# A new order of the second block's branches, and ten of its projection tiles in three FP32R passes

## The chip, the cores and the metric

The kernel runs on one core of a Trainium2 chip. The metric is the device time of one execution in microseconds, all inputs in HBM at the start and the output there at the end.

## What is computed

Two blocks follow each other on x, 256 tokens of 1024 channels, all in float32. The first is a hybrid layer (two attentions, a recurrence, spatial gating, four gated branch products and `merged @ w_out`). The second mixes with three branches and ends in a mixture of experts. Cut to what matters here:

```
hx = modulate(rmsnorm(x, norm1_g), mod[0], mod[1])
z  = hx @ w_in                       # hyena 768, HGRN 5*512 (q, f_fwd, f_bwd, i, g), Fourier 256 columns

# hyena: short convolution over tokens, then twice a product with a long bidirectional convolution
v, x1, x2 = split(short_conv3(z_hy)); h = hyena_filters(...)
y = x1 * fftconv(v, h[:, 0], h[:, 1]); y = x2 * fftconv(y, h[:, 2], h[:, 3]); y_hy = rmsnorm(y)

# HGRN: gated linear attention in both directions, 4 heads of 128
scores = einsum("bhtd,bhsd,bhtsd->bhts", q, k, decay);  o = scores @ v + carried state
y_hg = rmsnorm_per_head(o) * silu(g)

# Fourier: FFT over tokens and channels, real part, a small product
y_fn = rmsnorm(einsum(fftn(z_fn).real, fn_w) + fn_b)

x = x + mod[2] * (concat(y_hy, y_hg, y_fn) @ w_out)
h = modulate(rmsnorm(x), ...)
experts = router(h)                  # 2 of 16, within the best of 4 groups
x = x + mod[5] * sum over experts of combine * ((silu(h @ w_gate) * (h @ w_up)) @ w_down)
out = rmsnorm(x)
```

## The kernel before

One list, `PLAN`, names all jobs of the kernel: `("hg_set", 3)` is level 3 of HGRN's preparation. Each engine has its own functions for a job's name (`@part(TENSOR, "hg_set")` and so on), and each engine's program is made by walking through `PLAN` in order and emitting its part. Nothing reorders later: an engine does its jobs strictly in the order of `PLAN` and waits, at semaphores, for the jobs of others. `woven(main, fill)` puts one job of `fill` behind each job of `main`. The eight PSUM banks are handed out in turn in TensorE's order of jobs.

Activations lie with channels on the partitions. A weight matrix arrives in pieces of 2 MB (1024 x 512), each in one of three slots in SBUF; SyncE issues the loads in the order of first use in `PLAN`, and waits before each until the last user of the slot is done. One tile of a projection, `("channels", name, i)` (`tensor_channels`, L637), is 128 output channels x 256 tokens: eight fp32 matmuls of 128 x 256, each shown as two in the records. `("tokens", "v2", tt)` (L618) is the same for 128 tokens x 512. The names are f0, f1 (the forget gates), q2, v2, g2 (HGRN), hy0 (4 tiles), hy1 (2) and fn (2).

A product in three FP32R passes (`three_passes`, L1334 to L1336) splits both factors in a high and a low part, high x high, low x high and high x low: 24 matmuls per tile instead of 8, each faster than fp32. The high part of a weight tile is a copy by ScalarE (`scalar_split`, L1318), the low part is weight minus high by VectorE (`vector_split`, L1324), into a home in SBUF for the high part and over the weights in their slot for the low part. Before the change, out1, the first block's gated products and out2 are computed so.

The second block's mixer:

- `norm h2` makes the normed input; f0, f1 and q2 (12 tiles) are woven with the hyena filter: `filter_in` (L1538, a sine on ScalarE and VectorE between the two layers, L1562), `taps` (L1569) and `response` (L1596).
- `hg_start` (L1630, L1632 on VectorE) and `hg_diagonal` (scores of the diagonal). Then levels 0 to 7: `hg_set L` prepares the factors of a level on VectorE (six operations of 128x512: L1686, L1687, L1690, L1692, L1686, L1687) and GpSimd (two, L1698 and L1700, which prepare the second direction's state for the next level); `hg_scores L` is eight matmuls on TensorE (L1638) and two masked copies on VectorE (L1717). `sets` has two buffers, so set L waits for scores L-2.
- `hy_conv j` (VectorE, L1813 and twice L1816) is the short convolution of tile j, `hy_tokens n` turns it (L1827), `hy_freq o ft` is half of the forward transform (L1846; products L1860, L1861, L1863, L1864 on VectorE), `hy_time o` the inverse (L1877 or L1879; the gate L1889 or L1892).
- `fourier_in`, `fourier_turn`, `fourier_out` (L1902, L1919, L1934); `hg_out`, `hg_norm` (L1748, L1750, L1768), `hg_close` (Newton steps L506, L508, L510 on 128x1024, L1793, L1798).
- `norm2` (L1962) for hyena and Fourier; `cat_split` (ScalarE L1988, VectorE L1994) makes high and low parts of the branches' results for out2. `router_fold` (L2050), `out2` 0 to 7, `x_turn` (L2063, L2064).

In `PLAN` before, v2, g2, hy0, hy1, the convolutions and fn are the fill between the levels, and hyena's transforms, hg_out, hg_norm, norm2 and hg_close stand behind all of it.

Behind x_turn the router picks experts; the expert weights are loaded in an order that depends on its result, so SyncE waits for VectorE's L2648 before the first of them.

## Time and profile before

| | |
|---|---|
| median of 3 runs | 1199.16 us (1197.82 to 1199.33) |
| profiled execution, its time and its span | 1197.87 us, 1196.0 us |
| granted TensorE clock, mean of the span | 0.927 |
| TensorE busy | 1038.1 us (87%) |
| VectorE, ScalarE, GpSimd busy | 567.4 us (47%), 395.7 us (33%), 46.5 us (4%) |
| the chain that ended last | TensorE 72%, VectorE 13%, DMA 8%, ScalarE 4% |
| first projection tile of the second block | 610.75 us |
| last turn of x ends | 852.0 us |
| first load of an expert's weights issued | 869.92 us |
| hg_start on VectorE (L1630, L1632) | 0.70 + 1.23 us |
| router_fold on TensorE (L2050) | 1.85 us |
| a load of `w_in`, issue to landing, median | 8.3 us |

A span is the time from the first to the last recorded instruction of the profiled execution; durations and starts are all from that one execution. TensorE has two levels of clock, 1.2 and 2.4 GHz; the granted clock is the mean share of the higher one. Consecutive instructions overlap a little in the records, so the time of one in a row of many is the distance between starts, and the busy time of a row is slightly longer.

### The profile page before, as it was taken

The page shows a single profiled execution, that of the slowest core. Times are in us where ns is not written, and L with a number is a line of the kernel's source. Part 1 is how long each engine was busy: PE and PEld are TensorE (multiplying, and loading weights), DVE is VectorE, ACT ScalarE, POOL GpSimd, SP SyncE. Part 2 cuts the span into 40 slices and gives each one's busy share as a digit, 9 for nine tenths or more (in the row PEclk, how much of TensorE's full clock was granted, in tenths as well). Part 3 has the DMA queues.
Part 4 walks back from the last instruction along what each step waited for, and adds up shares of the span by engine and source line. Part 5 has one row for each costly group of instructions (what it writes and reads, how often), then busy time and mean ns, then how long its engine had stood idle before and what let it go on. Part 6 is the DMA issues. An engine that isn't in the chain of part 4 may idle for free.

```text
span 1196.0 us, 13332 instructions
## 1 busy us (share of the span) xinstructions
PE 1038.1 (87%) x5422; PEld 758.2 (63%) x5422; DVE 567.4 (47%) x1031; ACT 395.7 (33%) x664; POOL 46.5 (4%) x66
## 2 busy tenths in 40 slices
PE   5989897797879799989989995837788999999984
PEld 3465785564459689859967694736776565366531
DVE  2363324754345464515542167285584341277815
ACT  2222342643136454314351100212463230256501
POOL 1000000000000000000000022000000000000001
PEclk9999897899789899999989997978789999999988
DMA  9623163046971474356224213000187999799994
GB/s 303 185 93 107 47 224 129 1 141 229 387 298 71 141 253 158 140 198 208 71 94 141 95 48 140 1 1 1 58 333 301 325 349 387 291 404 409 408 388 158
DMA packets 110347, 230.63 MB, mean 193 GB/s; under 512 B 8236, under 2 KB 15693, under 8 KB 110286
## 3 DMA queue, kind: packets, MB, share of 16 engines
q1 hardware_dynamic: 104080, 216.44, 49.9%
q0 software_dynamic: 2880, 9.71, 2.1%
q10 hardware_dynamic: 3326, 3.63, 1.0%
q8 instruction: 43, 0.70, 0.2%
q14 instruction: 18, 0.15, 0.0%
HBM read 221.11 MB, written 8.65 MB: 192 GB/s over the span
## 4 chain that ended last, share of the span: by engine, by line
PE 72%; DVE 13%; DMA 8%; ACT 4%; issue 2%; POOL 0%; ACTq 0%; DVEq 0%; SPq 0%; POOLq 0%
PE bank L637 16%; PE bank L618 8%; PE bank L2398 5%; PE bank L1334 4%; PE bank L1335 4%; PE bank L1336 4%; PE bank L2337 4%; PE bank L2338 4%; PE bank L2339 4%; PE bank L2422 3%; DMA slot<-in_ada_w 3%; DMA more_slots<-in_moe_w_up 2%; DMA slot<-in_w_in 2%; PE bank L2330 2%; PE bank L1377 2%
## 5 line engine op out<-in xcount | busy, mean ns | idle before, releaser
L637 PE MATMUL bank<-x_and_h,slot 128*128 128x256 f32 x768 | 178.5, 390 | 4.9 <-ACT x_and_h L546 4.9
L637 PEld LDWEIGHTS bank<-x_and_h,slot 128*128 128x128 f32 x768 | 147.7, 195 | 32.2 <-issue 9.9
L1335 PE MATMUL bank<-rounded 128*128 128x256 f32 x480 | 136.2, 284 | 0.0
L1334 PE MATMUL bank<-rounded 128*128 128x256 f32 x416 | 121.5, 292 | 4.0 <-DVE slot_rounded L1324 4.0
L618 PE MATMUL bank<-slot,x_and_h 128*128 128x512 f32 x224 | 99.3, 601 | 4.5 <-DVE x_and_h L583 4.5
L1335 PEld LDWEIGHTS bank<-rounded 128*128 128x128 f32 x480 | 91.8, 191 | 0.3
L1336 PE MATMUL bank<-rounded,slot_rounded 128*128 128x256 f32 x296 | 84.3, 285 | 0.0
L1334 PEld LDWEIGHTS bank<-rounded 128*128 128x128 f32 x416 | 79.7, 192 | 6.3 <-issue 5.5
L1324 DVE TENSOR_TENSOR slot_rounded<-slot,rounded 128x1024 fp32r<-128x1024 f32 (+1 forms) x53 | 55.1, 1061 | 58.2 <-ACT rounded L1318 57.9
L618 PEld LDWEIGHTS bank<-slot,x_and_h 128*128 128x128 f32 x224 | 42.8, 193 | 56.1 <-issue 55.1
L647 ACT ACTIVATE arena<-bank 128x256 f32<-128x256 f32 x56 | 21.5, 385 | 145.3 <-PE bank L637 145.2
L1318 ACT ACTIVATE rounded<-slot 128x1024 fp32r<-128x1024 f32 (+1 forms) x53 | 47.5, 923 | 32.1 <-PE bank L1336 22.1
L2726 DVE TENSOR_TENSOR hidden<-hidden,bank 64x512 f32<-64x512 f32 (+3 forms) x19 | 12.9, 686 | 93.4 <-ACT hidden L2532 62.1
L1336 PEld LDWEIGHTS bank<-rounded,slot_rounded 128*128 128x128 f32 x296 | 57.1, 193 | 0.0
L2688 DVE TENSOR_TENSOR slot_rounded<-slot,weights_high 128x1024 fp32r<-128x1024 f32 x38 | 45.3, 1220 | 17.4 <-ACT weights_high L2499 17.0
L2499 ACT ACTIVATE weights_high<-slot 128x1024 fp32r<-128x1024 f32 x38 | 39.2, 1056 | 21.7 <-PE bank L2339 20.8
L1260 PE MATMUL bank<-slot,arena 128*32 128x512 f32 x192 | 30.4, 762 | 12.9 <-DMA slot<-in_ada_w 9.5
L2398 PE MATMUL bank<-more_slots,tokens_by_slot 128*64 128x512 f32 (+1 forms) x80 | 37.6, 626 | 3.6 <-DMA more_slots<-in_moe_w_up 3.6
L800 ACT ACTIVATE arena<-arena 128x128 f32<-128x128 f32 (+1 forms) x48 | 21.4, 447 | 56.7 <-DVE arena L792 56.6
L2532 ACT ACTIVATE hidden<-bank 64x512 f32<-64x512 f32 (+3 forms) x19 | 11.0, 588 | 88.1 <-PE bank L2399 81.4
L628 ACT ACTIVATE arena<-bank 128x512 f32<-128x512 f32 x16 | 9.5, 596 | 86.4 <-PE bank L618 86.4
L2399 PE MATMUL bank<-more_slots,tokens_by_slot 128*64 128x512 f32 (+1 forms) x80 | 37.7, 626 | 0.0
(485 smaller groups left out, 2027.4 us busy)
## 6 DMA issues: line engine op xcount, KB each, us to landing
slot<-in_w_in SPq DMA_DIRECT2D x27, 2048.0 KB, 8.3
slot<-in_ada_w SPq DMA_DIRECT2D x12, 2048.0 KB, 12.7
slot<-in_moe_w_down SPq DMA_DIRECT2D x11, 2048.0 KB, 16.4
more_slots<-in_moe_w_gate SPq DMA_DIRECT2D x8, 2048.0 KB, 16.1
more_slots<-in_moe_w_up SPq DMA_DIRECT2D x8, 2048.0 KB, 18.2
slot<-in_moe_w_gate SPq DMA_DIRECT2D x7, 2048.0 KB, 10.2
x_and_h<-in_moe_w_up SPq DMA_DIRECT2D x6, 2048.0 KB, 15.8
more_slots<-in_moe_w_down SPq DMA_DIRECT2D x5, 2048.0 KB, 17.2
```

Source lines behind the costliest of these rows:

```text
L618: mm = t.do.matmul(bank[:, :], h[:, k, tt * P:(tt + 1) * P], w[:, k, :], start=k == 0, stop=k == KT - 1)
L637: mm = t.do.matmul(bank[:, 0:S], w[:, k, i * P:(i + 1) * P], h[:, k, :], start=k == 0, stop=k == KT - 1)
L1318: a.do.activation(high, piece, ACT.Copy).then_inc(*inc("split_weights_high", q, name[0]))
L1324: v.do.tensor_tensor(low, piece, high.bitcast(F32), ALU.subtract).then_inc(*inc("split_weights_low", q, name[0]))
L1334: t.do.matmul(dst, w_hi, x_hi, start=start, stop=False)
L1335: t.do.matmul(dst, w_hi, x_lo, start=False, stop=False)
L1336: return t.do.matmul(dst, w_lo, x_hi, start=False, stop=stop)
L2337: t.do.matmul(dst, x_hi, high, start=start, stop=False)
L2338: t.do.matmul(dst, x_lo, high, start=False, stop=False)
L2339: return t.do.matmul(dst, x_hi, low, start=False, stop=stop)
L2398: gate = t.do.matmul(gate_bank[0:m, :], x[:, k, :], w_gate_r[:, k, :], start=k == 0, stop=k == KT - 1)
L2688: v.do.tensor_tensor(low, weights, high.bitcast(F32), ALU.subtract).then_inc(*inc("split_expert_low", i))
```

## The change

The diff's parts, cut to what matters. First the order of the jobs. `projections_start` is new, between out1 and the norm, and everything behind q2 is written out by hand:

```diff
+        PLAN += [merge[2][0], *[job for i in range(5) for job in (merge[2][i + 1], ("consts2", i))], *merge[2][6:], *[("out1", dt) for dt in range(KT)], ("projections_start",), ("norm_squares", "h2"), ("norm", "h2"), ("masks",)]
...
-        PLAN += woven([("hg_start",), ("hg_diagonal",), *[job for level in range(LEVELS + 1) for job in
-                                          (("hg_set", level), ("hg_scores", level))], ("hg_last_set",)],
-                      [*tokens("v2"), *channels("g2"), *channels("hy0"), *channels("hy1", 2), *[("hy_conv", j) for j in range(6)],
-                       *channels("fn", 2), ("fourier_in", 0), ("fourier_in", 1), ("fourier_turn",), ("fourier_out",)])
-        PLAN += [("hy_tokens", 0), ("hg_out", 0), ("hy_tokens", 1), ("hg_out", 1),
-                 ("hy_freq", 0, 0), ("hg_norm", 0), ("hy_freq", 0, 1), ("hg_norm", 1), ("hy_time", 0), ("norm2", "fn"),
-                 ("hy_freq", 1, 0), ("hg_close",), ("hy_freq", 1, 1), ("hy_time", 1), ("norm2", "hy")]
+
+
+        hy0, hy1, v2, fn, g2 = channels("hy0"), channels("hy1", 2), tokens("v2"), channels("fn", 2), channels("g2")
+        PLAN += [hy0[0], ("hg_start",), hy0[1], ("hy_conv", 0), ("hg_diagonal",), hy0[2], ("hg_set", 0), ("hy_conv", 1), ("hg_set", 1),
+                 ("hy_tokens", 0), ("hg_set", 2), ("hy_conv", 2), ("hg_scores", 0), ("hy_freq", 0, 0), ("hy_freq", 0, 1),
+                 ("hg_set", 3), ("hy_conv", 3), hy0[3], ("hg_scores", 1), hy1[0], ("hg_scores", 2), fn[0], ("hy_time", 0), ("hy_tokens", 1),
+                 ("hy_conv", 4), ("hg_set", 4), hy1[1], ("hg_set", 5), ("hg_scores", 3), ("hy_freq", 1, 0), ("hy_freq", 1, 1), fn[1],
+                 ("hg_scores", 4), ("hg_set", 6), ("hg_set", 7), v2[0], ("hg_scores", 5), v2[1], ("out2_start",), ("hg_last_set",),
+                 ("hg_scores", 6), ("fourier_in", 0), ("fourier_in", 1), ("hg_scores", 7), ("fourier_turn",), ("hy_conv", 5), ("hy_time", 1),
+                 ("hg_out", 0), ("norm2", "hy"), ("fourier_out",), ("hg_out", 1), ("hg_norm", 0), ("hg_norm", 1), ("norm2", "fn"),
+                 ("hg_close",), g2[0], g2[1], ("cat_split", "hy"), ("cat_split", "fn"), g2[2], g2[3], ("cat_split", "hg")]
-        PLAN.insert(PLAN.index(("norm2", "fn")) + 1, ("cat_split", "fn"))
-        PLAN.insert(PLAN.index(("hg_close",)) + 1, ("cat_split", "hg"))
-        PLAN.insert(PLAN.index(("norm2", "hy")) + 1, ("cat_split", "hy"))
-        PLAN.insert(PLAN.index(("hy_time", 0)), ("out2_start",))
```

Second, ten of the twelve tiles of f0, f1 and q2 (all but f0's first two) become three-pass products:

```diff
+        h2_high, h2_low = tiles_r(KT * S, KT), tiles_r(2 * KT * S, KT)
...
+
+        PROJECTIONS = [("channels", name, i) for name in ("f0", "f1", "q2") for i in range(4)][2:]
+
         @part(TENSOR, "channels")
         def tensor_channels(t, name, i):
+            job = ("channels", name, i)
             h, h_done = CHANNELS[name][0:2]
-            bank, w = psum.take(t, ("channels", name, i)), loads_view[name]
-            t.wait_ge(*loaded(name))
-            for k in range(KT):
-                t.wait_ge(*at(h_done, k))
-                mm = t.do.matmul(bank[:, 0:S], w[:, k, i * P:(i + 1) * P], h[:, k, :], start=k == 0, stop=k == KT - 1)
+            bank, w = psum.take(t, job), loads_view[name]
+            if job in PROJECTIONS:
+                high, _, low, _ = pieces(job)[0]
+                t.wait_ge(*at("split_h2_low", 1))
+                t.wait_ge(*at("split_weights_low", SPLITS.index(job), name))
+                for k in range(KT):
+                    mm = three_passes(t, bank[:, 0:S], high[:, k, :], low[:, k, :], h2_high[:, k, :], h2_low[:, k, :], k == 0, k == KT - 1)
+            else:
+                t.wait_ge(*loaded(name))
+                for k in range(KT):
+                    t.wait_ge(*at(h_done, k))
+                    mm = t.do.matmul(bank[:, 0:S], w[:, k, i * P:(i + 1) * P], h[:, k, :], start=k == 0, stop=k == KT - 1)
...
+        def split_beside(name, i):
+
+            job = ("channels", name, i)
+            if job not in PROJECTIONS or PROJECTIONS.index(job) + 2 >= len(PROJECTIONS):
+                return None
+            return PROJECTIONS[PROJECTIONS.index(job) + 2]
+
+        @part(SCALAR, "projections_start")
+        def scalar_projections_start(a):
+            for job in PROJECTIONS[0:2]:
+                scalar_split(a, job)
+
+        @part(VECTOR, "projections_start")
+        def vector_projections_start(v):
+            for job in PROJECTIONS[0:2]:
+                vector_split(v, job)
+
+        @part(VECTOR, "channels")
+        def vector_channels(v, name, i):
+            if (name, i) == ("f0", 0):
+                for half in range(2):
+                    x = slice(4 * half, 4 * half + 4)
+                    v.wait_ge(*at("split_h2_high", half))
+                    v.do.tensor_tensor(h2_low[:, x, :], hT[:, x, :], h2_high[:, x, :].bitcast(F32), ALU.subtract).then_inc(*inc("split_h2_low", half))
+            if split_beside(name, i):
+                vector_split(v, split_beside(name, i))
 
         @part(SCALAR, "channels")
         def scalar_channels(a, name, i):
             dst, func, free_after = CHANNELS[name][2:]
+            if (name, i) == ("f0", 0):
+                for half in range(2):
+                    x = slice(4 * half, 4 * half + 4)
+                    a.wait_ge(*at("h2", 4 * half + 3))
+                    a.do.activation(h2_high[:, x, :], hT[:, x, :], ACT.Copy).then_inc(*inc("split_h2_high", half))
+            if split_beside(name, i):
+                scalar_split(a, split_beside(name, i))
             for signal in free_after:
                 a.wait_ge(*at(*signal))
             a.wait_ge(*at("channels", name, i))
...
+            if job[0] == "channels":
+                _, name, i = job
+                high = HOMES["channels"][PROJECTIONS.index(job) % 3]
+                return [(high[0], *(v[name][:, :, i * P:(i + 1) * P] for v in (loads_view, rounded_view)), name)]
```

The waits of `scalar_split` go by three homes for these ten (a home is free when the tile three before it is done). Third, `cat_high` moves, since its old home is still read by g2, and its copies wait for hyena's last products instead of fn; out2 takes the branches in another order; the memsets at the edges of the short convolution's input move on GpSimd from `hy_conv` 0 to `hg_start`:

```diff
-        cat_low, cat_high = tiles_r(0, KT), hT_r
+        cat_low, cat_high = tiles_r(0, KT), tiles_r(3 * KT * S, KT)
...
-            a.wait_ge(*at("channels", "fn", 1))
+            a.wait_ge(*at("hy_products", 1, 1))
...
-            for n, k in enumerate((6, 7, 2, 3, 4, 5, 0, 1)):
+            for n, k in enumerate((0, 1, 6, 7, 2, 3, 4, 5)):
```

Since loads follow first use, their order becomes hy0, hy1, fn, v2, g2, out2 (before: v2, g2, hy0, hy1, fn, out2). Line numbers move: L637 becomes L650, L618 L620, L1638 L1697, L1846 L1904, L1827 L1885, L1877 L1935, the set's L1686/1687/1690/1692 become L1745/1746/1749/1751, L1717 L1776, L1813/L1816 L1871/L1874, L1324 L1383, L1334 to L1336 L1393 to L1395.

TensorE's order behind the last tile of q2. Before (L637 projection tile, L618 half of v2, L1638 diagonal, then levels), and where the levels end:

```order
L637 MATMUL bank<-x_and_h,slot 128x256 x16
L618 MATMUL bank<-slot,x_and_h 128x512 x8
L1638 MATMUL bank<-arena 128x128 x8
L618 MATMUL bank<-slot,x_and_h 128x512 x8
L637 MATMUL bank<-x_and_h,slot 128x256 x8
L1638 MATMUL bank<-arena 128x128 x8
L637 MATMUL bank<-x_and_h,slot 128x256 x16
```

```order
L637 MATMUL bank<-x_and_h,slot 128x256 x8
L1638 MATMUL bank<-arena 128x128 x24
L637 MATMUL bank<-x_and_h,slot 128x256 x16
L1902 MATMUL bank<-arena 128x2x128 x4
L1919 MATMUL bank<-arena 128x256 x8
L1934 MATMUL bank<-arena 128x256 x2
L1827 MATMUL bank<-ident,arena 128x128 x4
```

After (L650 tile, L1885 hy_tokens, L1697 diagonal and levels, L1904 two hy_freq, L1935 hy_time):

```order
L650 MATMUL bank<-x_and_h,slot 128x256 x16
L1697 MATMUL bank<-arena 128x128 x8
L650 MATMUL bank<-x_and_h,slot 128x256 x8
L1885 MATMUL bank<-ident,arena 128x128 x4
L1697 MATMUL bank<-arena 128x128 x8
L1904 MATMUL bank<-arena 128x256 x8
L650 MATMUL bank<-x_and_h,slot 128x256 x8
L1697 MATMUL bank<-arena 128x128 x8
L650 MATMUL bank<-x_and_h,slot 128x256 x8
L1697 MATMUL bank<-arena 128x128 x8
L650 MATMUL bank<-x_and_h,slot 128x256 x8
L1935 MATMUL bank<-arena 128x256 x8
```

Each pair of levels had one filler behind it before, and the last three groups of scores stand together with none; now both transforms and a turn stand between the levels.

VectorE's order from hg_start's last operation: before (L1632, set 0, the masks of level 0, set 1):

```order
L1632 TENSOR_TENSOR arena<-arena 128x1024
L1686 TENSOR_TENSOR arena<-arena 128x512
L1687 TENSOR_TENSOR arena<-arena 128x512
L1690 TENSOR_TENSOR arena<-arena 128x512
L1692 TENSOR_TENSOR arena<-arena 128x512
L1686 TENSOR_TENSOR arena<-arena 128x512
L1687 TENSOR_TENSOR arena<-arena 128x512
L1717 COPY_PREDICATED arena<-arena,bank 128x512 x2
L1686 TENSOR_TENSOR arena<-arena 128x256x2
```

and after (L1689 and L1691 hg_start, L1871/L1874 hy_conv 0, set 0, hy_conv 1):

```order
L1689 TENSOR_SCALAR arena<-arena 128x1024
L1691 TENSOR_TENSOR arena<-arena 128x1024
L1871 TENSOR_SCALAR arena<-arena,par 128x256
L1874 SCALAR_TENSOR_TENSOR arena<-arena,par 128x256 x2
L1745 TENSOR_TENSOR arena<-arena 128x512
L1746 TENSOR_TENSOR arena<-arena 128x512
L1749 TENSOR_TENSOR arena<-arena 128x512
L1751 TENSOR_TENSOR arena<-arena 128x512
L1745 TENSOR_TENSOR arena<-arena 128x512
L1746 TENSOR_TENSOR arena<-arena 128x512
L1871 TENSOR_SCALAR arena<-arena,par 128x256
L1874 SCALAR_TENSOR_TENSOR arena<-arena,par 128x256 x2
```

The masks of level 0 no longer stand between set 0 and set 1; the convolutions do. Sets 0, 1 and 2 all come ahead of the masks now.

VectorE at the end of hg_close, before (L510 the last Newton step, L1994 a split, L1860 to L1864 hyena's last products):

```order
L510 SCALAR_TENSOR_TENSOR arena<-arena 128x1024
L1793 SCALAR_TENSOR_TENSOR arena<-bank,par,arena 128x256 x4
L1798 TENSOR_TENSOR arena<-arena 128x256 x4
L1994 TENSOR_TENSOR rounded<-arena,x_and_h_rounded 128x1024
L1860 TENSOR_TENSOR arena<-bank,arena 128x512
L1861 TENSOR_TENSOR arena<-bank,arena 128x512
L1863 TENSOR_TENSOR arena<-arena 128x256
L1864 TENSOR_TENSOR arena<-arena 128x256
```

and after (L2052 are the splits of all three branches, L2094 the first of router_fold):

```order
L510 SCALAR_TENSOR_TENSOR arena<-arena 128x1024
L512 SCALAR_TENSOR_TENSOR arena<-arena 128x1024
L1852 SCALAR_TENSOR_TENSOR arena<-bank,par,arena 128x256 x4
L1857 TENSOR_TENSOR arena<-arena 128x256 x4
L2052 TENSOR_TENSOR rounded<-arena,rounded 128x512 x2
L2052 TENSOR_TENSOR rounded<-arena,rounded 128x1024
L2094 TENSOR_SCALAR mods<-mods 128x8
```

Hyena's products stood behind hg_close; now they are long done when it runs.

## Rows read from the trace of the kernel before

**Rows 1.** Waits of SyncE's queue (who waited for whom: total us, times, longest).
```profile
SPq L2262 <- DVE arena L2648: 140.7, 1, 140.7
```

**Rows 2.** Windows: length, PE, PEld, DVE, ACT, POOL busy; granted clock, DMA share, GB/s.
```profile
728.00:752.50 24.50, 9.08 (x48) 8.60 (x49) 21.02 (x35) 0.80 (x2) 6.75 (x8) 0.65 0.24 86
790.00:817.00 27.00, 6.15 (x20) 4.50 (x18) 18.63 (x29) 3.17 (x4) 0.00 (x0) 0.62 0.00 0
```

**Rows 3.** TensorE's groups by line, 602 to 853 us: busy, mean ns, idle ahead.
```profile
L1638 PE MATMUL bank<-arena 128*128 128x128 f32 x144 | 21.0, 307 | 15.6 <-DVE arena L1687 15.6
L1334 PE MATMUL bank<-x_and_h_rounded,rounded 128*128 128x256 f32 x64 | 18.7, 293 | 3.6 <-DVE rounded L1994 2.3 <-DVE slot_rounded L1324 1.3
L1538 PE MATMUL bank<-arena,par 33*64 33x256 f32 (+1 forms) x4 | 1.3, 394 | 0.5 <-ACT arena L1562 0.5
L1879 PE MATMUL bank<-arena 128*128 128x256 f32 x16 | 5.4, 507 | 19.6 <-DVE arena L1864 19.6
L1877 PE MATMUL bank<-arena 128*128 128x256 f32 x16 | 3.7, 385 | 1.4 <-DVE arena L1864 1.4
L1919 PE MATMUL bank<-arena 128*128 128x256 f32 x16 | 3.7, 383 | 0.8 <-ACT arena L1909 0.8
L1934 PE MATMUL bank<-arena 128*128 128x256 f32 x4 | 1.1, 398 | 0.8 <-ACT arena L1926 0.8
L1962 PE MATMUL bank<-arena,ones 128*128 128x256 f32 x8 | 2.1, 388 | 1.5 <-ACT arena L1953 1.5
```

**Rows 4.** Timeline of TensorE: start us, us, what [idle before].
```profile
651.38 3.62 PE L637 MATMUL bank<-x_and_h,slot 128*128 128x256 f32 x16
654.83 1.88 PE L1596 MATMUL bank<-arena 128*128 128x512 f32 x4
668.63 7.03 PE L618 MATMUL bank<-slot,x_and_h 128*128 128x512 f32 x16
...
739.46 3.78 PE L1638 MATMUL bank<-arena 128*128 128x128 f32 x16 [8.27 <-DVE arena L1687]
749.26 3.47 PE L1638 MATMUL bank<-arena 128*128 128x128 f32 x16 [6.02 <-DVE arena L1687]
...
819.88 0.36 PE L1334 MATMUL bank<-x_and_h_rounded,rounded 128*128 128x256 f32 x1
```

**Rows 5.** Timeline of ScalarE and VectorE in out1.
```profile
593.91 1.06 ACT L1318 ACTIVATE rounded<-slot 128x1024 fp32r<-128x1024 f32 x1 [1.77 <-PE bank L1336]
...
596.74 1.06 ACT L1318 ACTIVATE rounded<-slot 128x1024 fp32r<-128x1024 f32 x1 [1.77 <-PE bank L1336]
...
597.83 1.23 DVE L1324 TENSOR_TENSOR slot_rounded<-slot,rounded 128x1024 fp32r<-128x1024 f32 x1 [0.67 <-ACT rounded L1318]
```

**Rows 6.** Timeline of VectorE.
```profile
734.52 1.01 DVE L1816 SCALAR_TENSOR_TENSOR arena<-arena,par 128x256 f32<-128x256 f32 x2
...
739.76 2.35 DVE L1816 SCALAR_TENSOR_TENSOR arena<-arena,par 128x256 f32<-128x256 f32 x2
...
795.17 1.22 DVE L506 TENSOR_TENSOR arena<-arena 128x1024 f32<-128x1024 f32 x1
```

**Rows 7.** VectorE's groups by line, 667 to 817.5 us.
```profile
L1686 DVE TENSOR_TENSOR arena<-arena 128x512 f32<-128x512 f32 x16 | 11.0, 690 | 0.3
L1717 DVE COPY_PREDICATED arena<-arena,bank 128x512 f32<-128x512 uint8 x14 | 10.1, 728 | 26.9 <-PE bank L1638 26.9
...
L1860 DVE TENSOR_TENSOR arena<-bank,arena 128x512 f32<-128x512 f32 x4 | 2.8, 689 | 22.3 <-PE bank L1846 22.3
...
L1813 DVE TENSOR_SCALAR arena<-arena,par 128x256 f32<-128x256 f32 x6 | 2.4, 408 | 2.4 <-POOL arena L1807 2.4
...
L1793 DVE SCALAR_TENSOR_TENSOR arena<-bank,par,arena 128x256 f32<-128x256 f32 x4 | 1.7, 477 | 0.0
L1798 DVE TENSOR_TENSOR arena<-arena 128x256 f32<-128x256 f32 x4 | 1.4, 421 | 0.0
```

**Rows 8.** Timeline of GpSimd.
```profile
739.48 1.16 POOL L1698 TENSOR_TENSOR arena<-arena 128x512 f32<-128x512 f32 x1 [8.02 <-DVE arena L1687]
```

More of the change, by code:

```diff
@@ L1290, in build @@
         MERGES = [job for job in PLAN if job[0] == "merge"]
-        SPLITS = MERGES + [("out1", dt) for dt in range(KT)] + [("out2", dt) for dt in range(KT)]
+        SPLITS = MERGES + [("out1", dt) for dt in range(KT)] + PROJECTIONS + [("out2", dt) for dt in range(KT)]
         BRANCHES = list(dict.fromkeys(n for _, n, _ in MERGES))
@@ L1317, in scalar_split @@
                 a.wait_ge(*loaded(name))
-                a.do.activation(high, piece, ACT.Copy).then_inc(*inc("split_weights_high", q, name[0]))
+                a.do.activation(high, piece, ACT.Copy).then_inc(*inc("split_weights_high", q, topic_of(name)))
         def vector_split(v, job):
@@ L1798, in vector_hg_close, with gpsimd_hy_edges @@
                 v.do.tensor_tensor(cat[:, 2 + h, :], cat[:, 2 + h, :], pk[0][:, h, :], ALU.mult).then_inc(*inc("cat_hg", h))
-        @part(GPSIMD, "hy_conv")
-        def gpsimd_hy_conv(g, j):
-            if j == 0:
-                g.wait_ge(*at("response", 1, 1))
-                g.wait_ge(*at("taps_summed", 1, 1))
-                for c in (0, S + 1):
-                    g.do.memset(z_hy[:, :, c:c + 1], 0.0).then_inc(*inc("hy_edges"))
+        @part(GPSIMD, "hg_start")
+        def gpsimd_hy_edges(g):
+            g.wait_ge(*at("response", 1, 1))
+            g.wait_ge(*at("taps_summed", 1, 1))
+            for c in (0, S + 1):
+                g.do.memset(z_hy[:, :, c:c + 1], 0.0).then_inc(*inc("hy_edges"))
         @part(VECTOR, "hy_conv")
```

21 lines of the change are left out of this document (14 added, 7 removed).

## The prediction

> **What bounds the kernel now.** I started at the end and went backwards. Who holds the last third? The weight loads of the experts wait for the router's order: SyncE's queue sat 140.7 us behind VectorE's L2648 [rows 1], and the first gate matrix is issued at 869.92 us, right behind it. The change touches nothing behind that point, so whatever the second block saves up to there shifts all that follows as one piece. The change acts in the stretch from the first projection tile (610.75 us) to the last turn of x (852 us).
>
> Second, the granted clock: 0.65 in 728 to 752.5 us and 0.62 in 790 to 817 us [rows 2], where TensorE is busy 9.08 of 24.5 and 6.15 of 27 us. Third, the groups by line on TensorE over the whole stretch [rows 3]: their idle times are 15.6 (scores behind hg_set) + 19.6 and 1.4 (hyena's inverse transform behind its products) + 3.6 (out2's start) + 1.5 + 0.8 + 0.8 + 0.5 = 43.8 us. The 4.9 us ahead of the first tile (the norm) aren't touched. The rest of the stretch is full of matmuls, so TensorE is the floor, and only two things can give time: those idle times, and fewer TensorE cycles.
>
> Fourth, single instructions [rows 4]. The score groups of 739.46 and 749.26 stand 9.8 us apart with 8.27 and 6.02 us of idle time ahead: by then every projection had been used as filler, and each level waits for VectorE. The 19.6 us ahead of L1879 [rows 3] are VectorE's as well: hg_close's six steps on 128x1024 (1.23 us each) [rows 6] stand in its program ahead of hyena's last products.
>
> **The change, part by part.**
>
> *New order.* The same matmuls are issued, but the projection tiles are spread between the levels, both pairs of hyena transforms lie inside the levels, and the four g2 tiles cover hg_close. If all idle time goes: 43.8 us.
>
> *Clock.* Three groups ran at half clock behind gaps of 6 us and more: 3.78 and 3.47 us where full speed gives 1.95 (9 groups are 21.0 us in all [rows 3]; without these two 13.75 / 7 = 1.96), and L1879's 5.4 where as many of the same shape, L1877, take 3.7 [rows 3]. That is 1.83 + 1.52 + 1.7 = 5.0 us, back when no gap of that size is left.
>
> *Three passes.* A tile in fp32 takes 3.45 us (651.38 to 654.83) [rows 4]. Out1's tiles, whose 24 passes are the same, follow at 2.83 us: their splits on ScalarE, each waiting for a tile, start at 593.91 and 596.74 [rows 5]. Ten tiles: 6.2 us. New work for it: ten weight splits, ScalarE 1.06 and VectorE 1.23 us each [rows 5], two tiles ahead, and the split of h2 (two halves each). ScalarE and VectorE have 2.3 us of this per 2.83 us tile, on two engines that were mostly free there. The first two splits stand between out1 and the norm, while VectorE waits for the sum of squares: they cost nothing; without that cover they would cost 2 x 1.23. The split of h2 runs while tiles 0 and 1 are computed in fp32 (6.9 us against 2 x 1.06 + 2 x 1.23, from the same rows).
>
> Gross: 43.8 + 5.0 + 6.2 = 55.0 us.
>
> *New waits.* (a) Hyena's filter is a chain over ScalarE and VectorE, between shorter tiles now; it waits 0.5 us today (L1538 [rows 3]). I take 0.9 in place of none; bounds 0 and 1.9 (0.5 plus two or three tiles shorter by 0.62).
> (b) The turn of hyena's channels, hy_tokens 0, wants on VectorE hg_start (2.0), two hy_conv, set 0: about 9 us against 8.7 of TensorE (two tiles and the diagonal): 0.4.
> (c) The balance up to hy_tokens 1 decides. TensorE: six tiles 20.7, four groups of 1.8 = 7.2 (1.95 busy, and neighbours overlap by 0.17 as the tiles do), two pairs of transforms 7.0, a turn 0.4: 35.3 us. VectorE: hg_start 2.0, four sets of 6 x 0.69 less overlap = 16.0, masks 3 x 1.4, products 4.2, four hy_conv of 0.4 + 1.0 [rows 6, 7]: 32.1. GpSimd has two steps per level, of 1.16 us [rows 8]; today 12 of 16 fall where VectorE idles, now nearly all fall on its work. What that costs VectorE one pair of rows shows: L1816 twice is 1.01 us alone and 2.35 beside both GpSimd steps [rows 6], 0.67 per step. Eight steps: 5.3, so 37.4 against 35.3. I take 1.9; bounds 0 (no holding) and 6.3 (each step holds VectorE for its whole 1.16 us: 32.1 + 9.4 = 41.5).
> (d) Levels 4 to 7: VectorE has 25.5 + 5.3 = 30.8 against TensorE's 33.8: none.
> (e) Out2's start: VectorE must do fn's and hg_close's Newton steps (2.6 + 7.4), L1793 and L1798 (3.1 [rows 7]), the splits of the branches (2.6 and 1.06 on ScalarE), about 17.9 with handovers, against 13.8 of g2 + 1.9 of router_fold + 1.4 of out2's first four k: 0.8, and a weight split late by as much as now (0.8): 1.6; another 0.4 at a later tile. Bounds 0 and today's 3.6.
> Together 0.9 + 0.4 + 1.9 + 1.6 + 0.4 = 5.2 us.
>
> The Trainium skill ("SBUF — State Buffer", section "Who interferes with whom") says that a VectorE instruction with two SBUF inputs contends with a GpSimd instruction that reads SBUF, and that on the shared port pair the other side "fully blocks". The direction agrees with the 2.35 us; read strictly it gives the upper bound of (c) and so the second rival.
>
> *Not counted*: the other loading order (the queue has long idle spells here; 24% of DMA at 728 to 752.5 [rows 2]), hy_edges' memsets, cat_high's new place. Their cover is that TensorE has hy0's weights before q2 ends; without it up to one load's time would show, 8.3 us at the median.
>
> **Sum.** 55.0 - 5.2 = 49.8. The profiled execution took 1197.87 us (span 1196.0, 1.9 around it): 1148.1. The median of the runs shown is 1.3 above it: **1149 us**.
> Check from the other side: from 668.63 to out2's start at 819.88 [rows 4] are 151.3 us; less 39.7 idle and 5.0 of clock, 106.6 of work. Q2 would end at 668.6 - 6.2 + 0.9 - 0.5 = 662.8, and with 2.3 of waits out2 starts at 771.7, 48.2 earlier; its start saves 3.6 - 2.0 more: 49.8.
>
> **Rivals.**
> 1. *GpSimd locks VectorE fully* (chance 0.18). (c) is 6.3, and (d) becomes 25.5 + 9.4 - 33.8 = 1.1; 5.5 us more: 1155. For it: the quoted rule, and 0.67 is from one pair of instructions that may have overlapped in part. Against it: the rows show 0.67.
> 2. *No new wait* (0.14): VectorE's holding is absorbed since GpSimd's steps are not awaited at once: 1149 - 5.2 = 1144.
> 3. *The passes save nothing* (0.04): the chain of ScalarE (1.06), VectorE (1.23) and the filter's own steps gets longer than a tile, 2.83; TensorE waits as long as it saves: 1149 + 6.2 = 1155. Against it: out1 ran 8 tiles so without a wait.
> 4. *Slower: levels run in series behind VectorE* (0.02). If a level takes longer on VectorE and GpSimd than its filler on TensorE, fillers don't cover and each of 7 steps costs the 9.8 us between the two groups [rows 4] beside all other work: 106.6 - 17.6 (groups) + 2.0 + 68.6 + 5.3 (holding) = 164.9; out2 starts at 662.8 + 164.9 = 827.7, 7.8 late, less 1.6 at its start: 1205. It decides when a level needs over 9 us on VectorE; its set, mask and holding are 4.0 + 1.4 + 1.3, and products come on top at only two levels. So it is unlikely.
>
> **How the numbers follow.** The forecast has 0.62. The range takes in no new wait at all with an out1-like saving (1144) less the 3 us by which latencies and small terms can add up: 1141; upwards 1155 plus 5 for both mid cases together: 1160. A measurement of this kernel tells about 0.2% (2.4 us) from no change; all cases but the last are far beyond it: faster 0.97; between, 0.01; slower 0.02.
>
> **What would show it.** Per step: the first out2 matmul near 772 us (profiled); granted clock near 1.0 from 616 us to there; idle on TensorE in the stretch below 7 us; tiles of f0 to q2 2.83 us apart; L1816 and the sets' L1745/L1746 longer than 0.5 and 0.69 beside GpSimd, the mean of L1745 telling my 0.67 from full locking; the wait at hy_tokens 1 near 2 us. I'm wrong if a new gap of over 2 us brings half clock back, if TensorE waits for L1383's splits in front of the tiles, or if the first expert load isn't issued about 50 us earlier.

## The result, and the profile after

The changed kernel takes 1149.7 us (median of 4 runs, 1146.38 to 1152.84) beside 1198.68 us before: a ratio of 0.959, 95% interval 0.9575 to 0.9605. The forecast was 1149, with a range of 1141 to 1160. Its profiled execution is the fastest of the four, 1146.38 us with a span of 1144.6, so instants of it are compared with those of before one by one, and the sum with the medians.

TensorE's timeline after the change: its first tile, the first matmul behind q2 (662.75), and every row of the stretch with idle time ahead of it (it answers to [rows 4]).

```profile
610.51 6.02 PE L650 MATMUL bank<-x_and_h,slot 128*128 128x256 f32 x16 [4.95 <-ACT x_and_h L548]
...
621.91 0.61 PE L1597 MATMUL bank<-arena,par 64*64 64x256 f32 x2 [1.15 <-ACT arena L1621]
...
662.75 7.07 PE L650 MATMUL bank<-x_and_h,slot 128*128 128x256 f32 x32
...
675.49 0.63 PE L1885 MATMUL bank<-ident,arena 128*128 128x128 f32 x4 [0.44 <-DVE arena L1874]
...
700.93 0.63 PE L1885 MATMUL bank<-ident,arena 128*128 128x128 f32 x4 [2.16 <-DVE arena L1874]
...
770.89 0.36 PE L1393 MATMUL bank<-rounded 128*128 128x256 f32 x1 [0.53 <-DVE rounded L2052]
...
793.11 0.38 PE L1393 MATMUL bank<-rounded 128*128 128x256 f32 x1 [0.46 <-DVE slot_rounded L1383]
```

Between the first tile and out2's start lie 160.4 us (610.51 to 770.89), where 209.1 lay (610.75 to 819.88). The groups by line answer to [rows 3]:

```profile
L1393 PE MATMUL bank<-rounded 128*128 128x256 f32 x144 | 43.9, 305 | 1.0 <-DVE rounded L2052 0.5 <-DVE slot_rounded L1383 0.5
L1697 PE MATMUL bank<-arena 128*128 128x128 f32 x144 | 17.5, 275 | 0.0
L1597 PE MATMUL bank<-arena,par 33*64 33x256 f32 (+1 forms) x4 | 1.3, 394 | 1.2 <-ACT arena L1621 1.2
L1885 PE MATMUL bank<-ident,arena 128*128 128x128 f32 x8 | 1.3, 279 | 2.6 <-DVE arena L1874 2.6
```

The scores (L1697) wait for nothing, and 144 of them take 17.5 us instead of 21.0: no half clock there. The idle time of the stretch is 1.2 + 2.6 + 1.0 = 4.8 us instead of 43.8. The windows (columns as in [rows 2]) show the clock at its upper level, 2.4 GHz, all through the levels, and where it fell to 1.2 GHz once more:

```profile
663.00:700.00 37.00, 35.33 (x196) 31.33 (x194) 34.27 (x48) 4.44 (x10) 10.27 (x8) 1.00 0.26 86
700.00:770.00 70.00, 69.07 (x351) 56.16 (x351) 58.68 (x90) 16.50 (x28) 9.72 (x9) 1.00 0.26 91
770.00:776.00 6.00, 5.47 (x33) 5.15 (x33) 4.72 (x10) 2.40 (x3) 0.00 (x0) 0.72 0.00 1
```

The loads of the experts start as much earlier as the mixer ends: SyncE waits 87.6 us for the router instead of 140.7 (the loads of w_out come later in its queue), and the first load is issued at 820.22 us instead of 869.92.

```profile
820.22 0.41 SPq L2335 DMA_DIRECT2D slot<-in_moe_w_gate  x1
```

That is 49.7 us. From there to the end are 324.4 us, 326.1 before: one piece that shifts, as forecast, plus 1.7 us in a part that the change doesn't touch; the last experiments bear on them.

VectorE's timeline, at the places that set the remaining waits (it answers to [rows 6]):

```profile
672.58 2.77 DVE L1874 SCALAR_TENSOR_TENSOR arena<-arena,par 128x256 f32<-128x256 f32 x2
...
679.32 2.02 DVE L1745 TENSOR_TENSOR arena<-arena 128x512 f32<-128x512 f32 x1
681.25 1.54 DVE L1746 TENSOR_TENSOR arena<-arena 128x512 f32<-128x512 f32 x1
...
685.83 2.79 DVE L1874 SCALAR_TENSOR_TENSOR arena<-arena,par 128x256 f32<-128x256 f32 x2
...
698.19 2.59 DVE L1874 SCALAR_TENSOR_TENSOR arena<-arena,par 128x256 f32<-128x256 f32 x2
```

and GpSimd's, beside the first of them (it answers to [rows 8]):

```profile
672.30 1.58 POOL L1757 TENSOR_TENSOR arena<-arena 128x512 f32<-128x512 f32 x1 [14.83 <-DVE arena L1746]
673.96 1.10 POOL L1759 TENSOR_TENSOR arena<-arena 128x512 f32<-128x512 f32 x1
```

Beside GpSimd's two steps L1874 twice takes 2.77, 2.79 and 2.59 us instead of 1.01, and a set's first L1745 and L1746 take 2.02 and 1.54 instead of 0.69 each.

### The profile page after: what moved, and what is told of

Read it like the earlier page. It is cut to its first block, busy times and chain, and to the rows that moved or that the text cites. A ratio compares the mean times of both kernels' runs of the same rounds, so it can differ in the third digit from the quotient of the medians.

```text
span 1144.6 us, 13539 instructions
## 1 busy us (share of the span) xinstructions
PE 1022.7 (89%) x5502; PEld 751.9 (66%) x5502; DVE 588.6 (51%) x1043; ACT 409.6 (36%) x678; POOL 48.2 (4%) x66
## 3 DMA queue, kind: packets, MB, share of 16 engines
q1 hardware_dynamic: 104080, 216.44, 52.2%
## 4 chain that ended last, share of the span: by engine, by line
PE 71%; DVE 14%; DMA 8%; ACT 4%; issue 2%; ACTq 0%; DVEq 0%; SPq 0%
PE bank L650 11%; PE bank L620 9%; PE bank L2456 6%; PE bank L1393 5%; PE bank L1395 5%; PE bank L1394 5%; PE bank L2395 4%; PE bank L2396 4%; PE bank L2397 4%; DMA slot<-in_ada_w 3%; PE bank L2480 3%; DMA more_slots<-in_moe_w_up 2%; DMA slot<-in_w_in 2%; PE bank L2388 2%; PE bank L1436 2%
## 5 line engine op out<-in xcount | busy, mean ns | idle before, releaser
L1393 PE MATMUL bank<-rounded 128*128 128x256 f32 x560 | 165.5, 296 | 4.8 <-DVE slot_rounded L1383 4.2
L1394 PE MATMUL bank<-rounded 128*128 128x256 f32 x560 | 158.8, 284 | 0.0
L650 PE MATMUL bank<-x_and_h,slot 128*128 128x256 f32 x608 | 142.2, 392 | 4.9 <-ACT x_and_h L548 4.9
L650 PEld LDWEIGHTS bank<-x_and_h,slot 128*128 128x128 f32 x608 | 117.7, 197 | 22.9 <-issue 6.4
L1395 PE MATMUL bank<-rounded,slot_rounded 128*128 128x256 f32 x440 | 125.3, 285 | 0.0
L1393 PEld LDWEIGHTS bank<-rounded 128*128 128x128 f32 x560 | 107.6, 192 | 12.0 <-issue 8.1
L1394 PEld LDWEIGHTS bank<-rounded 128*128 128x128 f32 x560 | 107.5, 192 | 1.3 <-issue 1.0
L1383 DVE TENSOR_TENSOR slot_rounded<-slot,rounded 128x1024 fp32r<-128x1024 f32 (+1 forms) x63 | 67.8, 1097 | 71.4 <-ACT rounded L1377 71.2
L620 PE MATMUL bank<-slot,x_and_h 128*128 128x512 f32 x224 | 99.3, 601 | 4.5 <-DVE x_and_h L585 4.5
L1395 PEld LDWEIGHTS bank<-rounded,slot_rounded 128*128 128x128 f32 x440 | 84.6, 192 | 0.0
L620 PEld LDWEIGHTS bank<-slot,x_and_h 128*128 128x128 f32 x224 | 42.8, 193 | 56.0 <-issue 55.1
L1377 ACT ACTIVATE rounded<-slot 128x1024 fp32r<-128x1024 f32 (+1 forms) x63 | 57.9, 944 | 33.6 <-PE bank L1395 23.5
L2456 PE MATMUL bank<-more_slots,tokens_by_slot 128*64 128x512 f32 (+1 forms) x80 | 37.0, 618 | 3.7 <-DMA more_slots<-in_moe_w_up 3.7
L836 DVE SCALAR_TENSOR_TENSOR arena<-bank,arena 128x256 f32<-128x256 f32 (+1 forms) x24 | 13.3, 556 | 50.5 <-PE bank L822 50.4
```

The lines of the kernel that those rows point to most:

```text
L620: mm = t.do.matmul(bank[:, :], h[:, k, tt * P:(tt + 1) * P], w[:, k, :], start=k == 0, stop=k == KT - 1)
L650: mm = t.do.matmul(bank[:, 0:S], w[:, k, i * P:(i + 1) * P], h[:, k, :], start=k == 0, stop=k == KT - 1)
L1377: a.do.activation(high, piece, ACT.Copy).then_inc(*inc("split_weights_high", q, topic_of(name)))
L1383: v.do.tensor_tensor(low, piece, high.bitcast(F32), ALU.subtract).then_inc(*inc("split_weights_low", q, topic_of(name)))
L1393: t.do.matmul(dst, w_hi, x_hi, start=start, stop=False)
L1394: t.do.matmul(dst, w_hi, x_lo, start=False, stop=False)
```

## The experiments

Each kernel is the change with one edit unless it says otherwise; each was timed beside the kernel before. "The change beside it" is the changed kernel in the same group of runs on the same chip.

**The change again, twice.** No edit; each stands in a group of runs on one chip, to compare others of that group with.

> The changed kernel itself, unchanged, once more, as the yardstick of the other three on this chip. Expected: about 1150 us (1146 to 1153 so far). Its trace also tells whether the short stretch of half clock at out2's start (772.2 to 775.6 us in the first trace, some 1.7 us lost behind a wait of only 0.5 us) belongs to the kernel or comes and goes. If it belongs to it, it stands at the same place again; if it comes and goes, it is elsewhere or absent, and the spread of the times has its reason there.

> The changed kernel once more, as the yardstick of the next two on the same chip: 1149.5 within 1.5.

Measured: 1149.46 us (1148.54 to 1152.93) and 1151.54 us (1149.6 to 1151.82), the second half a microsecond above what was expected. The waits stand in both traces again, 2.15 us at the second turn, 1.1 in the filter, 0.5 at out2's start. The half clock at out2's start is in neither: it comes and goes. In its place both have one behind the router (granted clock 0.72 in 865 to 877 us in both traces; more below).

**The order without the passes.**

```diff
-        PROJECTIONS = [("channels", name, i) for name in ("f0", "f1", "q2") for i in range(4)][2:]
+        PROJECTIONS = []
```

> The new order alone: all twelve tiles of f0, f1 and q2 in fp32 again, no splits of h2 and of these weights. By the sum, the passes are worth 6.2 us less 0.7 of a longer wait in the filter chain (1.15 measured against 0.45), 5.5 us: 1155. If the passes saved nothing here (the rival with 4 in 100), this kernel takes 1149 to 1150. If the splits had cost the rest of the mixer something hidden, under 1153.

Measured: 1154.15 us (ratio to before 0.9626, 0.9607 to 0.9645), 4.7 above the change beside it. The intervals of the two ratios overlap (the change's is 0.9586 to 0.9617), so the trace has to carry this. From the first tile to out2's start this kernel takes 167.6 us, 7.2 more than the change:

```profile
612.13 6.03 PE L650 MATMUL bank<-x_and_h,slot 128*128 128x256 f32 x16 [4.95 <-ACT x_and_h L548]
...
622.85 0.61 PE L1597 MATMUL bank<-arena,par 64*64 64x256 f32 x2 [0.46 <-ACT arena L1621]
...
708.07 0.63 PE L1885 MATMUL bank<-ident,arena 128*128 128x128 f32 x4 [2.15 <-DVE arena L1874]
...
779.72 0.35 PE L1393 MATMUL bank<-rounded 128*128 128x256 f32 x1 [0.52 <-DVE rounded L2052]
```

Of these 7.2 us, 1.7 are a stretch of half clock behind the 2.15 us wait (709 to 713 us), which the change's traces don't have; 5.5 are left, as expected. The filter waits 0.46 us, as before the change [rows 3].

**The passes without the order.** The old order of jobs behind q2, the old home of `cat_high` and the old k in out2.

```diff
-        PLAN += [hy0[0], ("hg_start",), hy0[1], ("hy_conv", 0), ("hg_diagonal",), ...
+        PLAN += woven([("hg_start",), ("hg_diagonal",), ...], [*tokens("v2"), *channels("g2"), ...])
```

> The passes alone: ten tiles in three FP32R passes, but the old order of the branches behind q2, the old home of the high parts and the old order of k in out2. If the two parts add up, this gains what the new order alone (1154.15) left over: 4.7 to 5.5 us, so 1192 to 1193 beside 1197.7. If the shorter tiles are worth something only under the new order (for instance because the levels then reach their bare stretch earlier and wait more), under 4 us. The three groups of scores and hyena's inverse transform must show their 15.6 and 19.6 us of idle time again.

Measured: 1191.91 us beside 1199.28, a ratio of 0.9937 (0.9921 to 0.9953): 7.4 us, the interval reaching from 5.6 to 9.5, more than the 4.7 to 5.5 expected. The idle times are back (L1699 scores, L1939 hyena's inverse transform):

```profile
732.61 3.78 PE L1699 MATMUL bank<-arena 128*128 128x128 f32 x16 [7.14 <-DVE arena L1748]
742.41 3.78 PE L1699 MATMUL bank<-arena 128*128 128x128 f32 x16 [6.02 <-DVE arena L1748]
...
805.04 6.16 PE L1939 MATMUL bank<-arena 128*128 128x256 f32 x16 [19.56 <-DVE arena L1924]
```

The trace divides the gain otherwise than the expectation did. Counted from the first tile, q2 ends 5.6 us sooner and out2 begins 4.4 us sooner, but the first expert load comes only 1.9 us sooner: out2 waits 2.57 us for a split of the branches, and the clock is at its lower level behind that wait. From that load to the end, where nothing was changed, are 322.2 us instead of 326.1. So the parts add up roughly, 43.5 for the order alone, 4.7 to 7.4 for the passes, 48 to 49 for both, but 3.9 us of the 7.4 aren't the passes' own work.

**GpSimd's steps on VectorE.** Nothing runs on GpSimd between the levels.

```diff
-        @part(GPSIMD, "hg_set")
-        def gpsimd_hg_set(g, level):
...
+            v.do.tensor_tensor(b_lo, b_lo, e_hi, ALU.mult).then_inc(*inc("hg_state1"))
+            v.wait_ge(*now("hg_state1"))
+            v.do.tensor_tensor(a_hi, a_hi, e_lo, ALU.mult).then_inc(*inc("hg_state1", level))
```

> GpSimd's two steps of each hg_set are done by VectorE behind its own six, the rest as in the change. Theory (VectorE held by about 0.9 us per GpSimd step, as much as the step costs on VectorE itself or more): up to hy_tokens 1 VectorE has 8 x 0.65 = 5.2 us of work more and 7.3 us of holding less, so the waits ahead of the two turns (0.44 + 2.16 us) shrink to under 0.6, and the time falls by about 2 us or stays. Rival (the holding is an artefact of the records, GpSimd's help is real): VectorE is 5.2 us later at hy_tokens 1, the wait there grows to 7 us and the time by 5 us, with half clock behind it by 7.

Measured: 1147.74 us, 1.7 below the change beside it, and the waits of the turns are 0 and 1.01 us (expected: under 0.6) instead of 0.44 and 2.15:

```profile
701.28 0.63 PE L1881 MATMUL bank<-ident,arena 128*128 128x128 f32 x4 [1.01 <-DVE arena L1870]
```

VectorE does 16 more operations in all and is done sooner at both turns. The times alone wouldn't carry this (the ratios' intervals, 0.9561 to 0.9587 and 0.9586 to 0.9617, touch); the waits do. The rival, 5 us slower, is out: what looked like help costs VectorE at least as much as it takes off it.

**Convolution 3 ahead of set 3.**

```diff
-                 ("hg_set", 3), ("hy_conv", 3), hy0[3],
+                 ("hy_conv", 3), ("hg_set", 3), hy0[3],
```

> Only hy_conv 3 is put ahead of hg_set 3 on VectorE. hy_tokens 1 waited 2.16 us for this convolution, which stood behind set 3 (3.9 us) and was held by set 3's GpSimd steps (2.59 instead of 1.01 us). Theory (that wait was on the path, nothing else near it): the wait is gone, scores 3 come early enough, the time falls by 2.2 us. Rival (the wait moves one job on: the masks and the gate stand behind set 3 now, and scores 3 or the bank of hy_freq wait instead): no change within 0.5 us.

Measured: 1147.03 us, 2.4 below the change beside it. The turn waits for nothing now, but the next tile waits 0.67 us for a bank that the masks free, so a part of the wait moved on, as the rival had it, and the trace gives 1.5 us to this edit. The experts' part, untouched, took 326.6 us in this trace and 328.2 in that of the change beside it, of which more below:

```profile
700.41 0.60 PE L1885 MATMUL bank<-ident,arena 128*128 128x128 f32 x4
701.68 3.72 PE L650 MATMUL bank<-x_and_h,slot 128*128 128x256 f32 x16 [0.67 <-DVE arena L1776]
```

**The masks between the sets.** TensorE's program is unchanged; what changes is where the sets, the masks and the convolutions stand for VectorE and GpSimd.

```diff
-                 ("hy_tokens", 0), ("hg_set", 2), ("hy_conv", 2), ("hg_scores", 0), ("hy_freq", 0, 0), ("hy_freq", 0, 1),
-                 ("hg_set", 3), ("hy_conv", 3), hy0[3], ("hg_scores", 1), hy1[0], ...
+                 ("hy_tokens", 0), ("hg_scores", 0), ("hy_conv", 2), ("hg_set", 2), ("hy_freq", 0, 0), ("hy_freq", 0, 1),
+                 hy0[3], ("hy_conv", 3), ("hg_scores", 1), ("hg_set", 3), hy1[0], ...
...
-                 ("hy_conv", 4), ("hg_set", 4), hy1[1], ("hg_set", 5), ("hg_scores", 3), ...
+                 ("hy_conv", 4), ("hg_set", 4), hy1[1], ("hg_scores", 3), ("hg_set", 5), ...
...
-                 ("hg_scores", 4), ("hg_set", 6), ("hg_set", 7), v2[0], ("hg_scores", 5), v2[1], ...
+                 ("hg_scores", 4), ("hg_set", 6), v2[0], ("hg_scores", 5), ("hg_set", 7), v2[1], ...
```

> TensorE's program is that of the change, word for word; on VectorE the masks of scores, whose input is a PSUM bank, or hyena's products stand directly behind a set wherever they can, in place of the next set or a convolution, and conv 3 stands ahead of set 3. So less two-input work runs beside GpSimd's steps. Theory (VectorE is held only where it reads two inputs from SBUF): the masks and L1918/L1919 keep 0.73 and 0.68 us each beside GpSimd, L1745, L1746 and L1874 together lose most of their 10.9 us of extra time (to under 5), the waits at both turns go to 0.5 and under 0.3 us, and the time falls by 2 to 3 us against the change: 1146.5 to 1147.5. Rival (any VectorE instruction is held beside GpSimd): the masks take 1.3 us and more each, nothing is won over the kernel with conv 3 first (1147.0), and waits stay near 0.7 us or more.

> The kernel with the masks between the sets once more, to tell it from the change on one chip: if its waits of 2.15 us were the whole of it, it is 2.2 to 2.6 us faster than the change; it was 5.7 us below the change's time of another call, more than the trace accounts for (out2's start came 2.5 us earlier). If that was more than the spread between calls, it is again over 4 us faster.

Measured: 1143.73 us, below the expected 1146.5 to 1147.5, and 1144.33 us the second time, 7.2 below the change beside it (ratios to before 0.954, 0.9527 to 0.9553, and 0.9597, 0.9584 to 0.9611). What is held and what isn't, on VectorE:

```profile
678.35 1.36 DVE L1776 COPY_PREDICATED arena<-arena,bank 128x512 f32<-128x512 uint8 x2
679.60 0.57 DVE L1871 TENSOR_SCALAR arena<-arena,par 128x256 f32<-128x256 f32 x1
...
685.75 0.68 DVE L1918 TENSOR_TENSOR arena<-bank,arena 128x512 f32<-128x512 f32 x1
686.35 0.68 DVE L1919 TENSOR_TENSOR arena<-bank,arena 128x512 f32<-128x512 f32 x1
687.07 0.53 DVE L1921 TENSOR_TENSOR arena<-arena 128x256 f32<-128x256 f32 x1
687.51 1.37 DVE L1922 TENSOR_TENSOR arena<-arena 128x256 f32<-128x256 f32 x1
```

and the GpSimd steps beside them:

```profile
678.51 1.51 POOL L1757 TENSOR_TENSOR arena<-arena 128x512 f32<-128x512 f32 x1 [4.23 <-DVE arena L1746]
...
685.91 1.40 POOL L1757 TENSOR_TENSOR arena<-arena 128x512 f32<-128x512 f32 x1 [4.78 <-DVE arena L1746]
687.39 1.22 POOL L1759 TENSOR_TENSOR arena<-arena 128x512 f32<-128x512 f32 x1
```

The masks (L1776, data from a PSUM bank) take 1.36 us for two beside L1757, as alone. L1918 and L1919, one input from a bank, keep 0.68. L1922, both inputs in SBUF, takes 1.37 instead of 0.42. One kind of row doesn't fit the theory: L1871, which reads one tensor and two per-partition scalars from SBUF, takes 0.57 us here and 0.51 once more beside GpSimd's steps, 0.41 elsewhere. The extra time of L1745, L1746 and L1874 falls from 10.9 us to 4.3 (L1745 and L1746 11.9 each, L1874 8.3 in the groups by line, where 11.0, 11.0 and 5.8 stand without GpSimd). L1922 isn't in that sum: its four take 3.5 us here instead of 1.7, so about 6 us of holding are left, not 4.3. The second turn waits for nothing, and out2 begins 2.5 us sooner after the first tile (157.8 us instead of 160.4); convolution 3's place alone had given 1.6 of these. The wait was expected to be worth 2 to 3 us, and is; the other 4 to 5 us lie behind the router, where nothing was changed.

**Both: masks between, and GpSimd's steps on VectorE.**

> The order of the run before, and GpSimd's steps done by VectorE. If GpSimd's help is real as soon as two-input work is kept away from it, this kernel has 16 x 0.65 = 10.4 us more VectorE work with only a few us of holding less, and is the same or up to 2 us slower than the run before, with waits of TensorE at the turns again. If the help is worth nothing in any order, both take the same time within 0.5 us and neither has waits over 0.5 us there.

Measured: 1143.39 us (ratio to before 0.9536, 0.9518 to 0.9554; with GpSimd 0.9535, 0.952 to 0.9551). The same time, no wait at either turn; the second of the expected outcomes. Within what these times tell, some 2 us, GpSimd's help is worth nothing in either order, and nothing more waits for VectorE at the turns.

**Out2's old order of k.**

```diff
-            for n, k in enumerate((0, 1, 6, 7, 2, 3, 4, 5)):
+            for n, k in enumerate((6, 7, 2, 3, 4, 5, 0, 1)):
```

> The change with out2's old order of k (Fourier, HGRN, hyena). In the change out2 waits 0.53 us for hyena's split, which stands on VectorE behind hg_close, and runs four k before it needs HGRN's. Now it needs Fourier's first and HGRN's after two: the wait for HGRN's split (ends near 772.6 us) grows, in all about 1.8 us of waits at the first tile instead of 0.5 (reached at 770.4; two k are 0.7 us). If the order of k doesn't matter, the waits stay at 0.5.

Measured, in a single execution: 1149.78 us, waits of 1.13 and 0.21 us in the first tile instead of 0.53. The new order of k is worth 0.8 us; 1.3 was expected.

```profile
771.64 0.36 PE L1393 MATMUL bank<-rounded 128*128 128x256 f32 x1 [1.13 <-DVE rounded L2052]
...
772.80 0.58 PE L1393 MATMUL bank<-rounded 128*128 128x256 f32 x1 [0.21 <-DVE rounded L2052]
```

**The filter chain one tile later**, on top of the masks between the sets.

```diff
-        PLAN += woven([*channels("f0"), *channels("f1"), *channels("q2")], taps)
+        PLAN += [f0[0], taps[0], f0[1], f0[2], taps[1], f0[3]] + woven([*f1, *q2], taps[2:])
```

> The kernel with the masks between the sets, and hyena's filter chain one tile later: filter_in 1 stands behind the third tile, the taps behind f1's tiles, the responses behind q2's. In all traces of the change TensorE waited 1.1 us for the sine ahead of filter_in 1, since VectorE's two subtractions of the split of h2 (3.20 us beside GpSimd's cast) stood ahead of the sine's steps. Theory: that wait goes and no other comes in its place, 1.1 us faster than the run beside it. Rival: the chain's end is late now (the taps' or the responses' results, which hy_edges and hyena's products wait for), and a wait at hy_tokens 0 or the first products takes back what was won.

Measured: 1148.13 us (1147.14 to 1149.0), 3.8 *slower* than the 1144.33 of the kernel with the masks between, beside it. Yet neither theory holds. The wait in the filter is gone and none came in its place: out2 begins 156.7 us after the first tile instead of 157.8, 1.15 sooner, and the first expert load 205.2 instead of 207.0. The loss is behind that: from the first load to the end 328.7 us instead of 323.6. There the experts' part, which is the same, runs at another clock. Windows of the kernel with the masks between:

```profile
770.00:776.00 6.00, 6.00 (x41) 6.00 (x40) 4.20 (x8) 1.99 (x2) 0.00 (x0) 0.72 0.00 0
865.00:877.00 12.00, 9.53 (x46) 4.24 (x47) 4.23 (x6) 2.19 (x4) 0.00 (x0) 1.00 0.48 177
1107.00:1119.00 12.00, 11.80 (x48) 3.64 (x48) 0.68 (x1) 0.59 (x1) 3.92 (x4) 0.86 0.75 271
```

and of the one with the filter later:

```profile
770.00:776.00 6.00, 5.77 (x49) 5.59 (x50) 3.76 (x8) 2.12 (x2) 0.00 (x0) 1.00 0.00 0
865.00:877.00 12.00, 10.88 (x40) 4.22 (x40) 2.96 (x5) 1.19 (x2) 0.00 (x0) 0.72 0.42 171
1107.00:1119.00 12.00, 9.96 (x34) 2.71 (x36) 0.00 (x0) 0.03 (x1) 3.92 (x4) 0.72 0.86 319
```

**Needless work.** Ten passes more, on top of the later filter chain, so that all that follows stands where it stood in the kernel with the masks between.

```diff
+                for _ in range(10 if job == PROJECTIONS[0] else 0):
+                    t.do.matmul(bank[:, 0:S], high[:, 0, :], h2_high[:, 0, :], start=True, stop=True)
```

> The kernel with the filter chain one tile later, plus ten needless FP32R passes on TensorE ahead of the third tile (10 x 0.1175 = 1.2 us, overwritten by the tile's first pass), so that everything behind it stands where it stood in the kernel with the masks between (1144.3), though with work where that one waited. Theory (the 3.8 us by which the later filter lost, although out2 began 1.15 us sooner after the first tile, are stretches of half clock behind the router, 0.72 of the clock in 865 to 877 us and again near 1110, and whether they come depends on how the earlier work falls in time): with 1.2 us more of work it is faster than 1148.1 or at least not slower, near 1144 to 1146, and the clock in 865 to 877 us is 1.0 again. Rival (something in the later filter itself costs the experts' part 3.8 us): it is 1.2 us slower than before, 1149.3, with the same stretches of half clock.

Measured: 1145.0 us beside 1198.87 (ratio 0.9546, 0.9532 to 0.956; without the ten passes 0.9575, 0.9562 to 0.9588). More work, and 3.1 us less time, though in two groups of runs whose intervals only just part. The clock is back in 865 to 877 us, and lower at out2's start:

```profile
770.00:776.00 6.00, 5.49 (x34) 5.42 (x34) 4.79 (x10) 2.51 (x3) 0.00 (x0) 0.72 0.00 1
865.00:877.00 12.00, 8.90 (x44) 3.36 (x43) 3.95 (x6) 2.19 (x3) 0.00 (x0) 1.00 0.47 176
1107.00:1119.00 12.00, 10.68 (x42) 3.37 (x44) 0.68 (x1) 0.59 (x1) 4.44 (x5) 0.86 0.73 272
```

From the first load to the end are 323.4 us again. So the 3.8 us belonged to the instants at which work stood, not to the filter's place. Why the clock falls with the one set of instants and not with the other isn't shown.

## Why the prediction was right

**The bound and the shift** held. SyncE's first expert load moved by 49.7 us, out2's start by 48.75 measured from the first tile; forecast were 49.8 and 48.2.

**Idle time, 43.8 us**, went as listed: no group of scores and no transform waits. **Clock, 5.0 us**, came back in the levels: 3.5 us in the scores, and hyena's second inverse transform takes 3.6 us instead of 5.4. **Three passes, 6.2 us**: q2 ends 52.2 us after the first tile instead of 57.9 (662.75 - 610.51 against 668.63 - 610.75), 5.6 us, with 0.7 of a longer wait in it; forecast 5.8. The run without the passes gives 5.5 from its trace and 4.7 from its times.

**The new waits, 5.2 us**, measured in the forecast's order: 1.15 for 0.9, 0.44 for 0.4, 2.16 for 1.9, none for (d), 0.53 + 0.46 for 1.6 + 0.4. In all 4.7. Two of these were right with a wrong inside, and one was too high:

- Term (c) took 0.67 us of holding per GpSimd step, 5.3 in all. Measured are 1.76, 2.19, 1.78 and 1.58 us for the four pairs, 7.3. VectorE was at hy_tokens 1 after 37.3 us (663.47 to 700.78) all the same, the forecast's 37.4, since I had counted three pairs of masks ahead of convolution 3 and only one stands there (2.7 us less), and left out 1.5 us in which VectorE waited for hy0's first tile; the rest ran some 0.9 us shorter than counted. So the mechanism held, its size was 2.0 us too low, and that the wait met the forecast is luck. The run with GpSimd's steps on VectorE confirms the holding: VectorE had about 5 us more of its own work ahead of that turn, was done 1.4 us sooner, and the wait fell to 1.01 us. The masks between the sets don't bear on this wait, since convolution 3 ahead of set 3 took it away by itself.
- Term (a) was put down to shorter tiles. The trace shows another cause: the two subtractions that split h2 take 3.20 us beside GpSimd's cast, where two such subtractions take 2.46 alone, and the sine's first step stands behind them. The tiles ahead of this wait are f0's first two, in fp32 and no shorter than before; without the passes it was 0.46 us.

```profile
615.72 3.20 DVE L677 TENSOR_TENSOR rounded<-x_and_h,rounded 128x1024 fp32r<-128x1024 f32 x2 [3.13 <-ACT rounded L688]
618.84 0.53 DVE L1604 TENSOR_SCALAR arena<-bank,par 64x256 f32<-64x256 f32 x1
```

- Term (e) had 1.6 us where out2 waited 0.53: the weight split that was to be late by 0.8 held up nothing here, and 0.23 us in the two later traces of the change.

**The rivals.** Full locking (1155) is out as a time, and only half out in size: a pair of GpSimd steps takes 2.6 to 3.0 us and holds VectorE for 1.6 to 2.2, not for all of it, but the 7.3 us held lie halfway between the forecast's 5.3 and this rival's 9.4. That the wait of 6.3 us did not come is due to the miscounted masks as well. Its rule is right in kind, though: the Trainium skill ("SBUF — State Buffer", "Who interferes with whom") says that a VectorE instruction with two SBUF inputs contends with a GpSimd instruction that reads SBUF, and that one with at most one SBUF input, outside its two-port modes, does not. The masks, at 1.36 us for two, and the products from a bank, at 0.68 each, agree. The Trainium skill's "fully blocks" stands there for the two-port modes; the prediction carried it over to two inputs. The rival without any new wait (1144) has the number of the kernel with the masks between, but not its reason: that kernel still waits 2.5 us in the stretch, and its experts' part is 4 to 5 us shorter. That the passes save nothing and that levels run in series are both out: without the passes the first turn stands 5.5 us later after the first tile, and no level waits. Of the prediction's own signs of being wrong, a gap of over 2 us did come (2.16), but no half clock behind it; behind the same gap of 2.15 us in the kernel without the passes there was some.

**What the forecast didn't have** is the half clock at out2's start in one trace (from there to the first load 49.3 us, 48.5 in the two later traces of the change), and the 4 to 5 us by which the experts' part differs among kernels that don't touch it. The forecast took that part as unchanged. In the profiled execution it was 1.7 us shorter, 324.4 instead of 326.1; in the two later executions of the same kernel it was 328.2 and 328.4. So the shift of 49.7 us up to the first load is what the sum foresaw; that the whole time met the forecast within 1 us has luck in it as well. The first tile, ahead of which these kernels do nearly the same, starts anywhere from 609.7 to 613.0 us in the traces of the change and its variants. The four times of the change spread over 6.5 us; in the later groups it spread over 4.4 and 2.2, and the kernel before over 2.8 to 5.5, so the wide spread isn't a mark of the change.

The fastest versions are the two with the masks between the sets, 1143.7 and 1143.4 us, the second of them without GpSimd.
